# Two-block transformer kernel on one core: other PSUM banks for three tenants, and the rotary half-exchange by on-chip DMA

## The reference: two transformer blocks at batch 1, 256 tokens, width 1024, all in float32

```python
def reference(x, ...):
    # first block
    proj = rms_norm(x, attn_norm_g) @ w_in
    mq = rope(split_heads(proj[..., o_mq:o_mk], 8), pos)     # 8 heads of 64
    mk = rope(split_heads(proj[..., o_mk:o_mv], 8), pos)
    y_moba = merge_heads(moba_attention(mq, mk, mv))         # at 256 tokens: causal softmax attention
    y_gla = gla_attention(gq, gk, gv, log_a) ...             # gated linear attention, 4 heads
    x = x + concat([y_moba, y_gla]) @ w_out
    x = x + (silu(conv(h_gate)) * conv(h_val)) @ w_ffn_down
    x = rms_norm(x, final_norm_g)
    # second block: four branches (conv, spatial gate, stick-breaking, forgetting attention)
    merged = sum_n sigmoid(gate_n) * (y_n @ w_branch[n])
    x = x + merged @ w_out_2
    return x + swiglu(rms_norm(x), w_ffn_in_2, w_ffn_out_2)

def rope(t, pos):                                            # per head of 64 columns
    t1, t2 = t[..., : hd // 2], t[..., hd // 2:]
    return jnp.concatenate([t1 * cos - t2 * sin, t2 * cos + t1 * sin], axis=-1)
```

## Time and profile before

| | |
|---|---|
| median of 3 runs | 761.29 us (760.97 to 766.78) |
| the profiled execution's own time | 761.31 us |
| its span, first to last instruction | 759.5 us |
| PE busy | 742.2 us, 98% of the span |
| DVE, ACT, POOL busy | 68%, 49%, 6% |
| granted PE clock | 1.0 in the whole span |
| DMA | 128.25 MB, mean 169 GB/s |

### The profile page before, as it was taken

One profiled execution on the slowest core, in us unless ns is written; L12 is line 12 of the kernel. 1 busy time (PEld: TensorE's weight loads), 2 busy tenths in 40 slices (PEclk: granted clock), 3 DMA queues, 4 the chain that ended last, 5 costly groups with the idle time before them and its releaser, 6 DMA issues.

```text
span 759.5 us, 12109 instructions
## 1 busy us (share of the span) xinstructions
PE 742.2 (98%) x4858; PEld 666.3 (88%) x4858; DVE 513.9 (68%) x577; ACT 374.9 (49%) x441; POOL 45.8 (6%) x63
## 2 busy tenths in 40 slices
PE   8999998999999999999999999999999999999997
PEld 8899886788888888889989999899987888888886
DVE  4558748479888888876558636666576766665673
ACT  6534457455555455455664554534435444434331
POOL 2354200100000000030000000000010000000000
PEclk9999999999999999999999999999999999999999
DMA  8833432336655455435434444445543555555431
GB/s 317 331 111 113 167 111 103 120 111 229 215 169 204 179 193 195 167 111 173 160 125 154 167 167 167 167 167 180 207 169 111 188 200 174 214 169 204 180 111 55
DMA packets 18043, 128.25 MB, mean 169 GB/s; under 512 B 2000, under 2 KB 2256, under 8 KB 2768
## 3 DMA queue, kind: packets, MB, share of 16 engines
q1 hardware_dynamic: 18000, 127.63, 47.3%
HBM read 126.57 MB, written 1.05 MB: 168 GB/s over the span
## 4 chain that ended last, share of the span: by engine, by line
PE 90%; DVE 5%; ACT 2%; issue 1%; POOL 1%; DMA 1%; SPq 0%; DVEq 0%; ACTq 0%
PE ps L1427 21%; PE ps L1402 17%; PE ps L1403 17%; PE ps L1404 17%; PE ps L1433 11%; DVE low L923 1%; PE ps L1391 1%; DVE xx L971 1%; PE ps L1525 1%; DVE h L954 1%; DMA cst<-in_cst 1%; PE ps L1562 1%; ACT hiw L554 0%; PE ps L1534 0%; ACT xx L584 0%
## 5 line engine op out<-in xcount | busy, mean ns | idle before, releaser
L923 DVE TENSOR_TENSOR low<-raw,hiw 128x2048 fp32r<-128x2048 f32 x116 | 267.9, 2311 | 121.6 <-ACT hiw L554 120.8
L554 ACT ACTIVATE hiw<-raw 128x2048 fp32r<-128x2048 f32 x116 | 221.9, 1914 | 175.6 <-PE ps L1433 113.2
L1427 PE MATMUL ps<-xx,hiw 128*128 128x512 f32 x704 | 169.3, 391 | 1.4 <-DVE xx L971 1.2
L1427 PEld LDWEIGHTS ps<-xx,hiw 128*128 128x128 f32 x704 | 129.9, 188 | 29.8 <-DVE xx L971 3.5
L1402 PE MATMUL ps<-xx,hiw 128*128 128x256 f32 x512 | 146.8, 287 | 2.3 <-DVE arena L1352 1.7
L1403 PE MATMUL ps<-xx,hiw 128*128 128x256 f32 x512 | 144.8, 283 | 0.0
L1404 PE MATMUL ps<-xx,low 128*128 128x256 f32 x512 | 144.8, 283 | 0.0
L1402 PEld LDWEIGHTS ps<-xx,hiw 128*128 128x128 f32 x512 | 97.9, 191 | 4.3 <-DVE arena L1352 1.9
L1403 PEld LDWEIGHTS ps<-xx,hiw 128*128 128x128 f32 x512 | 97.9, 191 | 0.1
L1404 PEld LDWEIGHTS ps<-xx,low 128*128 128x128 f32 x512 | 97.9, 191 | 0.0
L1433 PEld LDWEIGHTS ps<-xx,low 128*128 128x128 f32 x704 | 90.3, 191 | 3.4
(11 more groups left out here) (198 smaller groups left out, 810.8 us busy)
## 6 DMA issues: line engine op xcount, KB each, us to landing
raw<-in_slabs SPq DMA_DIRECT2D x117, 1024.0 KB, 4.8
vec<-in_vec SPq DMA_DIRECT2D x1, 1258.5 KB, 9.8
cst<-in_cst SPq DMA_DIRECT2D x1, 1220.0 KB, 13.5
h<-in_x SPq DMA_DIRECT2D x2, 512.0 KB, 4.3
out<-h SPq DMA_DIRECT2D x2, 512.0 KB, 2.6
vec<-in_vec SPq DMA_DIRECT2D x1, 229.0 KB, 4.7
cst<-in_cst SPq DMA_DIRECT2D x1, 66.0 KB, 4.4
```

Of the source, the lines that this page charges most:

```text
L554: act.activation(hiw[:, n % SPLIT, :], raw[:, n % RAW, :], ACT.Copy).then_inc(hi_made, 1)
L923: dve.tensor_tensor(low[:, n % SPLIT, :], raw[:, n % RAW, :], hiw[:, n % SPLIT, :].bitcast(F32), ALU.subtract).then_inc(lo_made, 1)
L1427: pe.matmul(banks[:, c, :], hi[:, kt, cc_], xx[:, kt].rearrange("p a b -> p (a b)"), start=kt == 0, stop=False)
```

## The change

**Banks.** Level 0 goes to banks 2 and 5, `mo3` to bank 5, and `l2_1` and `l3_1` to banks 2 and 3. **Rotation.** The four `rotate` products and their tenants are gone. In their place SP issues four DMAs for each of mq0, mk0, mq1, mk1, 32 partitions x 512 float32 (64 KB) each, from `qpre` to a new buffer `qswap`, with neighbouring groups of 32 partitions exchanged. SP's loop over slabs is written out up to slab 11, and the DMAs stand behind the loads of slabs 7, 8, 10 and 11, after a wait for the evacuation. The sign that `C_ROT` held is put into `sin_signed`, which DVE makes once (a row sum of `C_ROT`, then a multiply of 128 x 256). DVE's second product now reads `qswap` and `sin_signed`, both in SBUF.

```diff
@@ tenants
-        for n in ("mq0", "mk0", "mq1", "mk1"):
-            tenant(n + "r", 7)
         for L in GLA_LEVELS:
             for par in range(2):
-                tenant(f"lev{L}_{par}", 3 + par)
+                tenant(f"lev{L}_{par}", (2, 5)[par] if L == 0 else 3 + par)
...
-                tenant(f"mo{hh // 2}", 7)
+                tenant(f"mo{hh // 2}", 5 if hh == 6 else 7)
...
-            tenant(f"l2_{m}", 4)
-            tenant(f"l3_{m}", 5)
+            tenant(f"l2_{m}", 2 if m == 1 else 4)
+            tenant(f"l3_{m}", 3 if m == 1 else 5)
@@ buffers
+        qswap = [piece(1024 + 512 * j, 2, T) for j in range(2)]
+        sin_signed = piece(7168, T)
@@ SP
-            for n in range(RAW, 2 * RAW):
+            for n in range(RAW, 4 * RAW):
                 sp.wait_ge(lo_made, n - RAW + 1)
                 sp.dma_start(raw[:, n % RAW, :], slabs_in[n]).then_inc(raw_full[n % RAW], 16)
-            sp.dma_start(vec[:, V_FIRST:], vec_in[:, V_FIRST:]).then_inc(s("vec_rest_in"), 16)
-            with sp.Fori(2, NS // RAW) as i:
+                if n == 2 * RAW - 1:
+                    sp.dma_start(vec[:, V_FIRST:], vec_in[:, V_FIRST:]).then_inc(s("vec_rest_in"), 16)
+                if IN1[n - 5] in ROPED:
+                    rope_i = ROPED.index(IN1[n - 5])
+                    sp.wait_ge(*given_back(IN1[n - 5]))
+                    if rope_i >= 2:
+                        sp.wait_ge(s("roped"), rope_i - 1)
+                    for b in range(4):
+                        sp.dma_start(qswap[rope_i % 2][32 * (b ^ 1):32 * (b ^ 1) + 32], qpre[rope_i % 2][32 * b:32 * b + 32])\
+                          .then_inc(s(f"swapped{rope_i}"), 16)
+            with sp.Fori(4, NS // RAW) as i:
@@ DVE
+            me.step(dve, dve.tensor_reduce(st[:, 34:35], C(C_ROT), AX_X, ALU.add))
+            me.step(dve, dve.tensor_scalar(sin_signed, C(C_SIN, T), st[:, 34:35], -1.0, ALU.mult, ALU.mult))
...
-                dve.wait_ge(*full(name + "r"))
-                dve.tensor_tensor(mrot, two(name + "r"), C(C_SIN, T).unsqueeze(1).broadcast_to([P, 2, T]),
-                                  ALU.mult).then_inc(*frees(name + "r"))
-                dve.wait_ge(*given_back(name + "r"))
+                dve.wait_ge(s(f"swapped{i}"), 64)
+                me.step(dve, dve.tensor_tensor(mrot, qswap[i % 2], sin_signed.unsqueeze(1).broadcast_to([P, 2, T]),
+                                               ALU.mult))
@@ PE
-            def rotate(name):
...
-                if IN1[k - 1] in ROPED:
-                    rotate(IN1[k - 1])
```

## The result

| | before | after |
|---|---|---|
| median | 761.13 us (760.86 to 766.78, 4 runs) | **753.48 us** (753.40 to 753.70, 4 runs) |
| profiled execution | 761.31 us, span 759.5 | 753.49 us, span 751.7 |

A forecast was written before the change was run, and what follows sets the result against it. PE, busy 742.2 of 759.5 us, was taken to bound the kernel. 3.76 + 1.2 + 1.2 + 1.86 - 0.8 = 7.22 us off 761.31 gave 754.1 us, range 752.9 to 756.2.

The forecast's parts named there:

- DVE and POOL: Rotary embeddings: two-SBUF-input DVE instructions alternate with POOL's, ending 0.6 to 0.9 us later each; 0.8 us lost in round 7.
- the wait for the probabilities: Sign in round 7: PE's one wait for DVE's probabilities grows from 1.1 us to 1.6 to 2.2.
- Rotations: Four rotation slots on PE, 0.94 us each, are removed and counted whole: 3.76 us gained.
- Level 128: PE no longer waits for DVE's reading of level 0 before level 128: 1.2 us gained, range 0.9 to 1.5.
- `mo3`: `moba_values(3)` no longer waits for DVE's reading of `mo2`, but then for ACT's turned probabilities: 1.2 us gained.
- `l2_1`: With new banks `l2_1` starts right behind the last product of m = 0: 1.86 us gained, counted whole.
- the middle instruction: Sign on DVE: the middle rotary instruction takes 1.1 to 1.4 us instead of 0.69.
- The exchange: The DMA exchange from `qpre` to `qswap` is hidden behind DVE's earlier work and SP's idle time: costs 0.
- the landing: Sign for the DMAs: exchanges land 3 to 6 us after issue, with no DVE wait for them.
- No toll: Rival: the middle rotary instruction meets no POOL instruction at the shared port; 753.0 to 753.3 us, chance 0.23.
- New waits: Rival: DVE late before the scores or POOL late for a level; 755 to 757 us, chance 0.18 shared with another rival.
- The exchange lands late: Rival: exchanges land at 13.5 us, delaying each rotary embedding 3.5 us; 768 us if nothing is absorbed, chance 0.04.

The follow-up runs named there:

- experiment 2: The changed kernel with the old bank lines, so only the exchange by DMA is new: 758.21 us.
- experiment 3: The kernel before, rotations kept, with DVE's middle rotary instruction reading `qpre` in SBUF instead of the rotated rows in PSUM: 761.63 us.
- experiment 4: The changed kernel without the 16 exchange DMAs and the waits for them, DVE reading `qpre` in place of `qswap`: 753.68 us.
- experiment 1: The kernel before with only the bank changes, rotations still on PE: 757.20 us.
- experiment 7: The changed kernel with each exchange issued one slab load later, also called the late exchange: 761.99 us.
- experiment 5: The changed kernel with DVE's fourth rotary embedding moved behind the probabilities of round 7: 752.05 us.
- experiment 9: The changed kernel with each exchange one slab load later, plus 8 and 14 products of zeros on PE ahead of its two waits: 757.69 us.
- experiment 8: The changed kernel with each exchange one slab load later, plus 13 and 26 products of zeros on PE ahead of its two waits: 761.47 us.
- experiment 6: The kernel before with DVE's fourth rotary embedding moved behind the probabilities of round 7, nothing else: 760.36 us.

## Where the prediction failed, and what of it was right

The forecast was 754.1 us and the time is 753.5: inside the range, with 0.6 us more gained than forecast. The prediction gave 0.68 to a change within 1% and 0.30 to faster by more. What was measured is 1.01% by the medians and 1.14% by the ratio (0.92 to 1.36%), so it is the faster side, which the prediction held for the less likely. The step that failed is the term for DVE and POOL: it took -0.8 us, with the wait for the probabilities growing from 1.1 to 1.9, and the runs show -0.45, with that wait at 1.55 (experiments 2, 3 and 4 all have it). The mechanism of the term was right and its size was not. With -0.45 in its place the sum is 7.57 us, right at the 1% line of 7.6, and the chances, drawn from a sum 0.4 us short of the line, had to come out otherwise. On which side of the line the medians fell is luck: of the 7.8 us in the traces 0.29 are the start's, and the change's own 7.5 us are 0.98%.

- **Rotations, 3.76: measured 3.44.** I took the slot from the rotation's start to the next, 0.94, and did not count that the level or the scores start 0.09 later behind a projection than the rotation did.
- **Level 128, 1.2: measured 1.44.** I held back 0.3 us for POOL's decays being pushed by the sine's two instructions. Without them level 128 follows level 0 by 1.14 us (experiment 1) and with them by 1.19: the push is 0.05 us.
- **`mo3`, 1.2: measured 1.18**, with the ACT wait of 0.63 us in its place. **`l2_1`, 1.86: measured 1.86.**
- **DVE and POOL, -0.8: measured -0.45.** This is the largest miss, and the step that failed. The alternation is real, and experiment 3 shows it with nothing else changed. I added 0.6 to 0.9 us for a rotary embedding. In round 7 the middle instruction takes 0.54 us longer (0.69 to 1.23), and the third, which alternated with POOL already, gives 0.09 back (1.31 to 1.22): together 0.45. I had charged the new alternation without setting off the one that was there before. The toll of the earlier rounds was absorbed, as I had put it.
- **The exchange, 0: measured 0** (experiment 4). I had 5 us of landing; it is 2.5 to 3.0 for three exchanges and 4.8 for the one right behind a slab load. SP's issues cost 0.6 us each, not 0.43, which nobody waits for.
- **The start, not in the sum: 0.29.** No term of the change; see above.

In the order of the terms: -0.32 + 0.24 - 0.02 + 0 + 0.35 + 0.29 = 0.54 us, the distance from the forecast gain of 7.2 to 7.8. Of the signs that were to show it right, three came out beside their ranges: the wait for the probabilities (1.55 us, not 1.6 to 2.2), the middle instruction (0.99 to 1.23, not 1.1 to 1.4) and the landing (from 2.5, not from 3).

The rivals. *No toll* is refuted in its mechanism, though its time of 753.0 to 753.3 lay nearer than my own; it ended 0.2 us below the result. *New waits* came up nowhere. *The exchange lands late* did not happen, but experiment 7 made it happen, and shows that I priced it wrongly in two ways that cancel in part: I let nothing be absorbed, where PE saw 3.7 of DVE's 11.0 us, and I had no clock in it, which took 4.3 us more. My break-even was 7.2 us of waits on DVE; with 11.0 of them the late exchange is 0.8 us slower than the kernel before.

## What to carry to other kernels

Read a removed instruction's worth as the distance between its neighbours in both versions, not as its own slot. Before an input is moved from PSUM to SBUF on DVE, look at what POOL does at the same time: here 0.69 us became 0.99 to 1.23, and the way out was to take the instruction off the path to the next PE wait (experiment 5), not to speed it up. A wait of PE is to be priced with the clock behind it (here such a stretch followed each of the waits of 1.86 to 3.39 us, and one of the shorter ones), and a filled wait can be cheaper than an idle one: 757.7 us against 762.0. But the fill must not be longer than the wait; with too many products nothing was gained.

## What the runs showed of the hardware that was not expected

- **An idle wait costs PE its clock behind it.** In the late exchange, waits of 1.89 and 3.39 us were followed by stretches at 0.50 of full clock, 1.2 GHz, which cost 1.5 and 2.8 us. PE's first wait for its inputs shows the same: where it took 1.86, 1.87, 1.97 and 2.39 us (experiments 7, 3, 9 and 8) the clock fell to 0.50 for a stretch behind it, and where it took 0.80 to 1.57 us (the seven other traces) it stayed at 1.00. It is seen in another place too: behind the wait of 1.78 us at `moba_values(3)` in one execution of experiment 6. Busy time and clock there:

```profile
128.00:134.00 6.00, 5.56 (x22) 4.34 (x23) 2.92 (x3) 1.37 (x2) 0.00 (x0) 0.72 0.88 303
```

- The clock did not fall behind every such wait: at the same place it stayed at 1.00 after 1.80 and 1.81 us in the traces of the kernel before and of experiments 2 and 3. The execution of experiment 6 took 761.76 us, the kernel's others mostly 760.0 to 760.5. The kernel before has the same wait and has such executions too (762.5 to 764 beside 761.1 to 761.3), and the changed kernel has neither in its four runs. But that wait can't be the whole cause: in experiment 1 it is 0.63 us, and four of its eight executions still are 1.5 us and more above the others. The wait at the start is the likelier one. The traces of experiments 3, 7, 8 and 9, in which the clock fell there, are of executions that took 1.2 to 2.1 us more than the median of their kernel. No run tried it by itself.
- **An on-chip transfer behind a slab load lands late.** 64 KB landed 2.5 to 3.0 us after issue where the last slab load had been issued 1.6 us or more before, and 4.8 us where the load of 1 MB was just ahead: in the changed kernel's third exchange, and 4.5 to 4.8 us in all four of the late exchange.
